# Turning the inner values of the last two experts ahead of the down products before them, in the mixture-of-experts stage of a four-layer diffusion trunk

## The chip, the cores and the metric

One Trainium2 chip, one core of it. The metric is the device time of one execution in microseconds (us), as a median over several runs. All data is 32-bit floating point; most products of the mixture-of-experts stage are computed in the type fp32r, with every operand split into an upper and a lower part.

## The reference

One inference step of a trunk with 4 layers, for 128 context tokens and 256 latent tokens (384 in all) of width 1024. Layer l has a token mixer (gated DeltaNet, grouped-query attention, latent attention, gated DeltaNet) and then a mixture of 16 experts in 4 groups of 4: each token is sent to its best group and to the best two experts in it. Both halves of a layer end in a residual and a layer norm. Cut to the part that the change touches:

```python
def _moe(h, router_w, router_b, w_gate, w_up, w_down):
    ...
    combine = jnp.einsum("tk,tke->te", w, jax.nn.one_hot(e_idx, N_EXPERTS, dtype=jnp.float32)).astype(h.dtype)
    hid = jax.nn.silu(jnp.einsum("td,edf->tef", t, w_gate)) * jnp.einsum("td,edf->tef", t, w_up)
    out = jnp.einsum("tef,efd->td", hid * combine[..., None], w_down)
    return out.reshape(B, N, D)
```

The inner width of an expert is 256. Every layer has its own expert weights.

## The kernel before

Five engines run programs of their own and meet by semaphores: SyncE (SP) issues the weight loads, TensorE (PE) multiplies, ScalarE (ACT) and VectorE (DVE) read the results out of PSUM, GpSimd (POOL) does small side work in the mixers. Weights come through a ring of 8 slots of 1 MB (`ring`, L375); SP's `load` (L662) waits until the slot is free (`ring_free`) and starts the transfer, in the order in which the products use them.

In the mixture-of-experts stage (`moe`, L1550 on TensorE, L2105 on ScalarE, L2839 on VectorE) the tokens of each group are gathered into a block of 128, and the four experts of the group work on this block. The stage is one hand-written list of steps, `MOE_STEPS` (L96 to L117), that TensorE goes through. A step is (kind, group, number):

- U: gate and up products of an expert (`gate_up`, L1538), in 4 pieces of weights with 6 matmuls each. Gate and up values lie in PSUM bank 0 or 1.
- T: the 128 x 256 inner values of an expert are turned (`transpose_hidden`, L1494), by two 128 x 128 transposes into one half of PSUM bank 2: experts with an even number use the first half, those with an odd one the second.
- D: down products of an expert (`down`, L1511), in 2 pieces of weights with 6 matmuls each. They add up in PSUM banks 3 and 4 over the four experts of the group.
- S: a scatter piece (`scatter_piece`, L1523): a quarter of a group's output is put back to its tokens.
- G and W: gathering the blocks, and the weights of the pairs of groups.

Experts of a layer are counted 0 to 15 in what follows: U15 is ("U", 3, 3), T14 is ("T", 3, 2), D13 is ("D", 3, 1). S2 and S3 are the last two scatter pieces of group 2, ("S", 2, 2) and ("S", 2, 3). Down products run two experts behind the gate and up products.

ScalarE and VectorE go through a second list, `MOE_FOLLOW` (L127 to L144), made out of the first one. A U or D step gives one entry P for each piece of weights, and the followers of the other steps (and the "u" of a U step) are collected and put in behind the second piece of the next U or D step. So the order of `MOE_STEPS` also sets the order of work on these two engines. The entries:

- P (pieces counted 0 to 95 in a layer; U15 has 86 to 89, D13 has 90 and 91, D14 92 and 93, D15 94 and 95): ScalarE writes the upper part of 1024 columns of weights (`split_high`, L2084, an activation at L1685, into `e_whi`), VectorE the lower part (`split_low`, L2813, L2817, into `e_wlo`). There are three buffers; ScalarE waits until the piece three before has been multiplied (`wfree`).
- u: ScalarE applies the SiLU to the gate values (L2092), VectorE multiplies by up values and routing weight (`hidden`, L2810), which gives the inner values.
- t: ScalarE copies the turned values out of bank 2 as the upper part (`hidden_t`, L2094, at L1685, semaphore `thi`), VectorE computes the lower part (`hidden_low`, L2819, L2822, semaphore `tlo`), into `e_hidT`. D waits for both.
- s: VectorE adds a scatter piece to the residual, 4 instructions (`scattered`, L2831, L2835).
- y: the group's output is copied in two parts (`y_high` at L1685, `y_low`, L2829).

The last steps of a layer are, on TensorE, `U15 S2 D13 S3 T14 D14 T15 D15` and then four scatter pieces of group 3. The list for the other two engines ends in `P88 P89 P90 P91 u15 s2 P92 P93 s3 t14 P94 P95 t15 y` and the four scatter pieces. Then the layer norm of the layer follows (L793, L1701, L2239), which needs all of them. Matmuls that belong together are written as three lines: L1505, L1508 and L1509 (`split_products`).

Of the kernel before, what the change touches and what calls it, by code (L numbers as in the profile page):

```python
# [29 lines left out]
D = 1024  # L30
KT = D // P
CTX, LAT = 128, 256
T = CTX + LAT
# [10 lines left out]
NE, NG, EPG = 16, 4, 4  # L44
# [51 lines left out]
MOE_STEPS = [("G", 0, m) for m in range(8)]  # L96
for _x in range(NE):
    _group, _turn = divmod(_x - 6, EPG)
    _late = _x >= 6 and _turn < 2
    if _x == 8:  # L100
        MOE_STEPS.append(("W", 1, 0))
    MOE_STEPS.append(("U", _x // EPG, _x % EPG))
    if _x == 0:
        MOE_STEPS.append(("W", 0, 0))
    if _x in (4, 5):
        MOE_STEPS += [("G", 1, 4 * (_x - 4) + m) for m in range(2)]
    if _late:
        MOE_STEPS.append(("S", _group, 2 * _turn))
    if _x >= 2:
        MOE_STEPS.append(("D", (_x - 2) // EPG, (_x - 2) % EPG))  # L110
    if _x in (4, 5):
        MOE_STEPS += [("G", 1, 4 * (_x - 4) + m) for m in range(2, 4)]
    if _late:
        MOE_STEPS.append(("S", _group, 2 * _turn + 1))
    if _x >= 1:
        MOE_STEPS.append(("T", (_x - 1) // EPG, (_x - 1) % EPG))
MOE_STEPS += [("D", 3, 2), ("T", 3, 3), ("D", 3, 3)] + [("S", 3, q) for q in range(4)]  # L117

MOE_UNITS = [(j, e, part) for kind, j, e in MOE_STEPS if kind in "UD" for part in ((0, 1) if kind == "U" else (2,))]

# [240 lines left out]
def trunk(nc, I, O):  # L361

    unit_at, n_units = unit_plan()
    with ExitStack() as ctx:
# [188 lines left out]
        def moe_sems(pre):  # L553
            names = "pick ga ga_ev whi wlo wfree sg hid tr thi tlo yhi ylo sc sc_ev".split()
            return dict(zip(names, sems(" ".join(pre + n for n in names))))

        F = moe_sems("f_")
# [173 lines left out]
        def _(pe):  # L731
# [714 lines left out]
            def gather_piece(l, pair, m):  # L1446

                at = 16 * l + 8 * pair + m
                half, q = divmod(m, 4)
                if m == 0:  # L1450
                    pe.wait_ge(F["pick"], 2 * l + pair + 1)
                    pe.wait_ge(tk_hi, 2 * TT * (l + 1))
                if m == 4:
                    pe.wait_ge(tk_lo, 2 * TT * (l + 1))
                if m >= 2:
                    pe.wait_ge(F["ga_ev"], at - 1)
                out = ps[:, 5 + q % 2, :].rearrange("p (g f c) -> p g f c", g=2, f=2)
                for f in range(2):
                    ft = 2 * q + f
                    for t in range(TT):  # L1460
                        last = mm(out[:, :, f, :], (e_hi, e_lo)[half][:, t, P * ft:P * ft + P], e_pick[:, t, :],  # L1461
                                  start=(t == 0), stop=(t == TT - 1))
                last.then_inc(F["ga"], 1)

            def pair_weights(l, pair, comb):

                pe.wait_ge(comb_ready, l + 1)
                pe.wait_ge(row2_ready, l + 1)
                for g in range(2):
                    at = EPG * (2 * pair + g)  # L1470
                    for t in range(TT):
                        last = mm(ps[:, 7, 96 + 4 * g:100 + 4 * g], e_pick[:, t, P * g:P * g + P].bitcast(F32),
                                  comb[:, t, at:at + EPG], start=(t == 0), stop=(t == TT - 1))
                last.then_inc(cs_mm, 1)
# [19 lines left out]
            def transpose_hidden(S, n, b):  # L1494

                pe.wait_ge(S["hid"], n + 1)
                for m in range(2):
                    last = nc.tensor.transpose(ps[:, 2, 256 * b + P * m:256 * b + P * m + P],
                                               e_hid[:, b, P * m:P * m + P], ident)
                last.then_inc(S["tr"], 1)  # L1500
# [10 lines left out]
            def down(S, n, p, e, k):  # L1511

                b = p % SPLITS
                pe.wait_ge(S["whi"], n + 1)
                pe.wait_ge(S["wlo"], n + 1)
                for y in range(2):
                    cols = slice(512 * y, 512 * y + 512)
                    last = split_products(ps[:, 3 + y, :], [e_hidT[:, e % 2, part, k, :] for part in range(2)],
                                          e_whi[:, b, cols], e_wlo[:, b, cols],
                                          e == 0 and k == 0, e == EPG - 1 and k == 1, S is F and p % 2 == 1 and y == 0)  # L1520
                last.then_inc(S["wfree"], 1)

            def scatter_piece(S, n, q, put, banks, first_of_two):  # L1523

                for ft in (2 * q, 2 * q + 1):
                    if ft % 4 == 0:
                        pe.wait_ge(S["yhi"], 2 * n + ft // 4 + 1)
                        pe.wait_ge(S["ylo"], 2 * n + ft // 4 + 1)
                    if ft >= len(banks):
                        pe.wait_ge(S["sc_ev"], n * KT + (ft - len(banks) + 1))  # L1530
                    elif first_of_two is not None:
                        pe.wait_ge(S["sc_ev"], first_of_two)
                    b = banks[ft % len(banks)]
                    mm(ps[:, b, 0:T], e_yhi[:, P * ft:P * ft + P], put, start=True, stop=False)
                    mm(ps[:, b, 0:T], e_ylo[:, P * ft:P * ft + P], put,
                       start=False, stop=True).then_inc(S["sc"], 1)

            def gate_up(S, n, p, j, e, k):  # L1538

                b = p % SPLITS  # L1540
                pe.wait_ge(S["whi"], n + 1)
                pe.wait_ge(S["wlo"], n + 1)
                for m in range(2):
                    kt, cols = 2 * k + m, slice(512 * m, 512 * m + 512)
                    last = split_products(ps[:, e % 2, :], [e_hs[:, j, part, kt, :] for part in range(2)],
                                          e_whi[:, b, cols], e_wlo[:, b, cols], kt == 0, kt == KT - 1,
                                          S is F and p % 2 == 1 and m == 0)
                last.then_inc(S["wfree"], 1)

            def moe(l):  # L1550
# [50 lines left out]
                with pe.If(crowded > 0):  # L1601
                    with pe.Fori(0, NG) as g:
                        for b in range(2):
                            n = g * 2 + (2 * NG * l + b)
# [30 lines left out]
                for kind, j, e in MOE_STEPS:  # L1635
                    n = NE * l + EPG * j + e
                    if kind == "G":
                        gather_piece(l, j, e)
                    elif kind == "W":
                        pair_weights(l, j, comb)  # L1640
                    elif kind == "U":
                        if e == 0 and j % 2 == 0:
                            pe.wait_ge(F["ga_ev"], 16 * l + 8 * (j // 2) + 8)
                        for k in range(4):
                            p = MOE_PIECE_OF["U", j, e, k]
                            gate_up(F, MOE_PIECES * l + p, p, HS_OF[j], e, k)
                    elif kind == "T":
                        transpose_hidden(F, n, e % 2)
                    elif kind == "D":
                        pe.wait_ge(F["thi"], n + 1)  # L1650
                        pe.wait_ge(F["tlo"], n + 1)
                        for k in range(2):
                            p = MOE_PIECE_OF["D", j, e, k]
                            down(F, MOE_PIECES * l + p, p, e, k)
                    else:
                        n = NG * l + j
                        if e == 0:
                            pe.wait_ge(F["ga_ev"], 16 * l + 16)
                        scatter_piece(F, n, e, e_put[:, j % 2, :], (6, 0, 1, 2) if j == NG - 1 else (5, 6),
                                      n * KT if n else None)  # L1660
# [9 lines left out]
            for l, kind in enumerate(KINDS):  # L1670
                {"gdn": gdn, "gqa": gqa, "mla": mla}[kind](l)
                layer_norm(2 * l, bufh, bufo, lambda k: pe.wait_ge(r_ready, KT * l + k + 1),
                           ("mid", l) if l + 1 < DEPTH else None)
                moe(l)
                layer_norm(2 * l + 1, bufx, bufh, lambda k: pe.wait_ge(F["sc_ev"], KT * (NG * l + NG - 1) + k + 1),
                           ("tail", l) if l + 1 < DEPTH else None)
# [1480 lines left out]
```

## Time and profile before

| | |
|---|---|
| median of 3 runs | 2187.74 us (2181.60 to 2188.81) |
| profiled execution, its own time | 2186.74 us |
| its span | 2184.9 us |
| TensorE busy | 2021.1 us, 92% |
| VectorE busy | 1338.0 us, 61% |
| ScalarE busy | 1034.3 us, 47% |
| granted TensorE clock, mean over the span | 0.973 |
| read from memory | 373.96 MB, 173 GB/s |

In a timeline a row gives the start in us from the start of the span, the duration in us, engine, line and operation, what is written and read, and how many instructions were merged into it (x2); in square brackets stands how long the engine had been idle before it, and what ended that. PEld is TensorE's weight load, which overlaps its matmuls. Ends of matmuls are modelled, and two in a row overlap: their pitch is taken from start to start. The granted clock is 1.00 at TensorE's full 2.4 GHz and 0.50 at 1.2 GHz.

### The profile page before, as it was taken

The page shows a single profiled execution, that of the slowest core. Times are in us where ns is not written, and L with a number is a line of the kernel's source. Part 1 is how long each engine was busy: PE and PEld are TensorE (multiplying, and loading weights), DVE is VectorE, ACT ScalarE, POOL GpSimd, SP SyncE. Part 2 cuts the span into 40 slices and gives each one's busy share as a digit, 9 for nine tenths or more (in the row PEclk, how much of TensorE's full clock was granted, in tenths as well). Part 3 has the DMA queues.
Part 4 walks back from the last instruction along what each step waited for, and adds up shares of the span by engine and source line. Part 5 has one row for each costly group of instructions (what it writes and reads, how often), then busy time and mean ns, then how long its engine had stood idle before and what let it go on. Part 6 is the DMA issues. An engine that isn't in the chain of part 4 may idle for free.

```text
span 2184.9 us, 44966 instructions
## 1 busy us (share of the span) xinstructions
PE 2021.1 (92%) x18880; PEld 1403.4 (64%) x18881; DVE 1338.0 (61%) x2625; ACT 1034.3 (47%) x1783; POOL 246.5 (11%) x363
## 2 busy tenths in 40 slices
PE   6999999898998999899899998998999999988996
PEld 3666666557775675677666665776466666647774
DVE  2656665437896342689822325898656666537896
ACT  3334344226774341676523315766444444326774
POOL 1422222110001000100010001000322232110000
PEclk8999999998999999899999998999999999999998
DMA  9244344345886444488644353888311121125880
GB/s 392 90 152 153 123 146 156 141 156 187 282 322 216 159 172 158 162 309 300 240 150 146 138 190 123 310 303 283 121 46 63 47 70 46 45 80 186 282 303 29
DMA packets 56912, 381.22 MB, mean 174 GB/s; under 512 B 6400, under 2 KB 10624, under 8 KB 12144
## 3 DMA queue, kind: packets, MB, share of 16 engines
q1 hardware_dynamic: 51696, 373.00, 47.7%
q10 hardware_dynamic: 4608, 4.20, 0.6%
q8 instruction: 159, 2.61, 0.5%
q0 software_dynamic: 384, 0.89, 0.1%
q14 instruction: 65, 0.53, 0.1%
HBM read 373.96 MB, written 4.10 MB: 173 GB/s over the span
## 4 chain that ended last, share of the span: by engine, by line
PE 76%; DVE 13%; ACT 5%; issue 4%; DMA 2%; ACTq 0%; SPq 0%; DVEq 0%
PE ps L838 15%; PE ps L1505 6%; DVE e_wlo L2817 5%; PE ps L1509 5%; PE ps L1508 5%; PE ps L788 4%; PE ps L764 4%; PE ps L744 3%; PE ps L979 3%; PE ps L1292 3%; DVE bufx L2835 2%; PE ps L799 2%; PE ps L1461 2%; ACT e_whi L1685 2%; PE ps L1393 2%
## 5 line engine op out<-in xcount | busy, mean ns | idle before, releaser
L2817 DVE TENSOR_TENSOR e_wlo<-ring,e_whi 128x1024 fp32r<-128x1024 f32 x384 | 456.2, 1222 | 90.9 <-ACT e_whi L1685 75.2
L1685 ACT ACTIVATE e_whi<-ring 128x1024 fp32r<-128x1024 f32 x384 | 402.9, 1060 | 117.9 <-PE ps L1509 114.4
L838 PE MATMUL ps<-bufh,ring 128*128 128x384 f32 x1024 | 392.4, 505 | 2.0 <-ACT scratch L1685 0.7
L838 PEld LDWEIGHTS ps<-bufh,ring 128*128 128x128 f32 x1024 | 177.0, 191 | 93.9 <-issue 18.3
L1505 PE MATMUL ps<-e_whi,e_hs 128*128 128x512 f32 x512 | 210.5, 411 | 28.2 <-DVE e_wlo L2817 24.8
L1685 ACT ACTIVATE scratch<-ps 128x384 f32<-128x384 f32 (+6 forms) x311 | 109.0, 368 | 213.2 <-PE ps L838 53.3
L1509 PE MATMUL ps<-e_whi,e_hs 128*128 128x512 f32 x512 | 200.4, 391 | 0.0
L1508 PE MATMUL ps<-e_wlo,e_hs 128*128 128x512 f32 x512 | 200.0, 391 | 0.0
L2946 POOL TENSOR_SCALAR bufx<-bufo,x_gb 128x384 f32<-128x384 f32 x56 | 37.6, 685 | 1072.5 <-DVE bufo L2256 1072.5
L1505 PEld LDWEIGHTS ps<-e_whi,e_hs 128*128 128x128 f32 x512 | 96.0, 188 | 69.1 <-ACT e_whi L1685 43.1
L2349 DVE SCALAR_TENSOR_TENSOR scratch<-scratch,par 128x386 f32<-128x386 f32 x192 | 128.5, 669 | 4.8
L744 PE MATMUL ps<-ring,silc 128*32 128x128 f32 x3072 | 106.3, 293 | 16.5 <-DMA ring<-in_w_ada 16.5
L1685 ACT ACTIVATE scratch<-ps,scratch 128x128 f32<-128x128 f32 x96 | 31.7, 365 | 189.3 <-PE ps L1139 187.7
L1505 PE MATMUL ps<-e_whi,e_hidT 128*128 128x512 f32 x256 | 102.0, 398 | 13.8 <-issue 9.2
L1509 PEld LDWEIGHTS ps<-e_whi,e_hs 128*128 128x128 f32 x512 | 96.1, 188 | 21.6
L1685 ACT ACTIVATE lnt<-ps 128x384 f32<-128x384 f32 x26 | 12.7, 490 | 200.6 <-PE ps L799 178.6
L744 PEld LDWEIGHTS ps<-ring,silc 128*32 128x32 f32 x3072 | 88.6, 117 | 29.7 <-issue 13.7
L1508 PEld LDWEIGHTS ps<-e_wlo,e_hs 128*128 128x128 f32 x512 | 96.4, 188 | 16.3
L979 PEld LDWEIGHTS ps<-scratch 32*32 32x32 f32 x6144 | 65.5, 108 | 55.9 <-issue 40.5
L1508 PE MATMUL ps<-e_wlo,e_hidT 128*128 128x512 f32 x256 | 100.8, 394 | 0.0
L1509 PE MATMUL ps<-e_whi,e_hidT 128*128 128x512 f32 x256 | 100.6, 393 | 0.0
L2235 DVE SCALAR_TENSOR_TENSOR bufh<-ps,mod,bufx 128x128 f32<-128x128 f32 x64 | 23.4, 412 | 118.9 <-PE ps L764 77.3
(312 smaller groups left out, 3490.7 us busy)
## 6 DMA issues: line engine op xcount, KB each, us to landing
ring<-in_moe SPq DMA_DIRECT2D x192, 1024.0 KB, 4.9
ring<-in_w_ada SPq DMA_DIRECT2D x96, 1024.0 KB, 6.8
ring<-in_gdn_w_in SPq DMA_DIRECT2D x32, 1024.0 KB, 7.0
ring<-in_gdn_w_out SPq DMA_DIRECT2D x8, 1024.0 KB, 5.0
ring<-in_gqa_w_in SPq DMA_DIRECT2D x6, 1024.0 KB, 5.1
ring<-in_gqa_w_out SPq DMA_DIRECT2D x4, 1024.0 KB, 6.9
ring<-in_mla_w_out SPq DMA_DIRECT2D x4, 1024.0 KB, 7.7
ring<-in_mla_w_in SPq DMA_DIRECT2D x3, 1024.0 KB, 4.9
```

Of the source, the lines that this page charges most:

```text
L744: last = mm(ps[32 * g:32 * g + 32, bank, 0:P], silc[:, kt, :], w[:, k, g, :], start=(kt == 0), stop=(kt == KT - 1))
L764: last = mm(ps[:, banks[t % len(banks)], 0:T], w[:, t % 2, kt, :], rhs[:, kt, :], start=(kt == 0), stop=(kt == KT - 1))
L788: last = mm(ps[:, banks[t % len(banks)], 0:T], w[:, t % 2, kt, :], bufo[:, kt, :], start=(kt == 0), stop=(kt == KT - 1))
L838: last = mm(ps[:, head_bank(n, m), 0:T], w[:, m % 2, kt, :], bufh[:, kt, :], start=(kt == 0), stop=(kt == KT - 1))
L979: last = mm(ps[quarter(g), bank, at:at + 32], g_inv[a][quarter(g), d, t, :], g_inv[b][quarter(g), d, t, :], start=True, stop=True)
L1292: last = mm(ps[:, bank, 0:T], w[:, pos % 2, kt, :], bufh[:, kt, :], start=(kt == 0), stop=(kt == KT - 1))
L1505: first = mm(out, parts[0], whi, start=start, stop=False)
L1508: mm(out, parts[0], wlo, start=False, stop=False)
L1509: return mm(out, parts[1], whi, start=False, stop=stop)
L1685: return op(out, in_, ACT.Copy, **kw)
L2349: done = stt(acc, g_cin[:, m, tap:tap + CONVW], taps[:, tap:tap + 1], acc, ALU.mult, ALU.add)
L2817: return tt_(e_wlo[:, b, :], w, e_whi[:, b, :].bitcast(F32), ALU.subtract)
```

## The change

T14 and T15 move forward in the list of steps, and TensorE gets one wait more in front of a T step (not for the first expert of a group): that the lower part of the expert before has been computed, since the two halves of bank 2 belong to one bank.

```diff
@@ -104,17 +104,21 @@
         MOE_STEPS.append(("W", 0, 0))
     if _x in (4, 5):
         MOE_STEPS += [("G", 1, 4 * (_x - 4) + m) for m in range(2)]
+    if _x == NE - 1:
+        MOE_STEPS.append(("T", NG - 1, EPG - 2))
     if _late:
         MOE_STEPS.append(("S", _group, 2 * _turn))
     if _x >= 2:
         MOE_STEPS.append(("D", (_x - 2) // EPG, (_x - 2) % EPG))
     if _x in (4, 5):
         MOE_STEPS += [("G", 1, 4 * (_x - 4) + m) for m in range(2, 4)]
+    if _x == NE - 1:
+        MOE_STEPS.append(("T", NG - 1, EPG - 1))
     if _late:
         MOE_STEPS.append(("S", _group, 2 * _turn + 1))
-    if _x >= 1:
+    if 1 <= _x < NE - 1:
         MOE_STEPS.append(("T", (_x - 1) // EPG, (_x - 1) % EPG))
-MOE_STEPS += [("D", 3, 2), ("T", 3, 3), ("D", 3, 3)] + [("S", 3, q) for q in range(4)]
+MOE_STEPS += [("D", 3, 2), ("D", 3, 3)] + [("S", 3, q) for q in range(4)]
@@ -1645,6 +1649,8 @@
                             p = MOE_PIECE_OF["U", j, e, k]
                             gate_up(F, MOE_PIECES * l + p, p, HS_OF[j], e, k)
                     elif kind == "T":
+                        if e:
+                            pe.wait_ge(F["tlo"], n)
                         transpose_hidden(F, n, e % 2)
```

The tail on TensorE becomes `U15 T14 S2 D13 T15 S3 D14 D15`, the list of the other two engines `P88 P89 P90 P91 u15 t14 s2 P92 P93 t15 s3 P94 P95 y`. The order of the weight pieces, and with it the order of the loads, stays as it is. This is so in all four layers.

## Rows read from the trace of the kernel before

**Rows 1.** The page, busy time, share of the span and instructions of each engine.
```profile
PE 2021.1 (92%) x18880; PEld 1403.4 (64%) x18881; DVE 1338.0 (61%) x2625; ACT 1034.3 (47%) x1783; POOL 246.5 (11%) x363
```

**Rows 2.** Timeline of TensorE, tail of layer 3: start us, us, engine, line, operation.
```profile
2141.16 0.33 PE L1534 MATMUL ps<-e_put,e_yhi 128*128 128x384 f32 x1
...
2141.87 0.40 PE L1505 MATMUL ps<-e_whi,e_hidT 128*128 128x512 f32 x1
...
2144.63 0.33 PE L1534 MATMUL ps<-e_put,e_yhi 128*128 128x384 f32 x1
...
2145.33 0.38 PE L1498 MATMUL ps<-con,bufh 128*128 128x128 f32 x2
2148.02 0.47 PE L1505 MATMUL ps<-e_whi,e_hidT 128*128 128x512 f32 x1 [2.31 <-issue]
...
2150.83 0.38 PE L1498 MATMUL ps<-con,bufh 128*128 128x128 f32 x2
2152.42 0.47 PE L1505 MATMUL ps<-e_whi,e_hidT 128*128 128x512 f32 x1 [1.21 <-ACT e_hidT L1685]
```

**Rows 3.** Timeline of VectorE, the same tail.
```profile
2136.65 0.41 DVE L2822 TENSOR_TENSOR e_hidT<-ps,e_hidT 128x256 fp32r<-128x256 f32 x1
...
2142.24 0.48 DVE L2810 SCALAR_TENSOR_TENSOR bufh<-ps,e_cs,bufh 128x256 f32<-128x256 f32 x1
2142.63 1.38 DVE L2835 SCALAR_TENSOR_TENSOR bufx<-ps,mod,bufx 128x128 f32<-128x128 f32 x4
2143.93 2.35 DVE L2817 TENSOR_TENSOR e_wlo<-ring,e_whi 128x1024 fp32r<-128x1024 f32 x2
2146.20 1.39 DVE L2835 SCALAR_TENSOR_TENSOR bufx<-ps,mod,bufx 128x128 f32<-128x128 f32 x4
2147.50 0.41 DVE L2822 TENSOR_TENSOR e_hidT<-ps,e_hidT 128x256 fp32r<-128x256 f32 x1
2147.84 1.22 DVE L2817 TENSOR_TENSOR e_wlo<-ring,e_whi 128x1024 fp32r<-128x1024 f32 x1
```

**Rows 4.** Timeline of ScalarE, the same tail.
```profile
2141.36 0.38 ACT L2092 ACTIVATE bufh<-ps 128x256 f32<-128x256 f32 x1 [0.30 <-PE ps L1509]
2141.64 1.05 ACT L1685 ACTIVATE e_whi<-ring 128x1024 fp32r<-128x1024 f32 x1
2143.46 1.06 ACT L1685 ACTIVATE e_whi<-ring 128x1024 fp32r<-128x1024 f32 x1 [0.76 <-PE ps L1509]
2145.75 0.38 ACT L1685 ACTIVATE e_hidT<-ps 128x256 fp32r<-128x256 f32 x1 [1.23 <-PE ps L1498]
...
2155.44 1.08 ACT L1685 ACTIVATE e_yhi<-ps 128x512 fp32r<-128x512 f32 x2 [3.81 <-PE ps L1509]
```

**Rows 5.** Timeline of TensorE, tail of layer 0: its D14 and D15 begin.
```profile
673.15 0.47 PE L1505 MATMUL ps<-e_whi,e_hidT 128*128 128x512 f32 x1 [2.31 <-issue]
...
677.56 0.47 PE L1505 MATMUL ps<-e_whi,e_hidT 128*128 128x512 f32 x1 [1.21 <-ACT e_hidT L1685]
```

**Rows 6.** Tail of layer 2, TensorE; then engines by window (PEclk, DMA share, GB/s last).
```profile
1518.03 0.47 PE L1505 MATMUL ps<-e_whi,e_hidT 128*128 128x512 f32 x1 [2.29 <-issue]
...
1522.23 0.60 PE L1498 MATMUL ps<-con,bufh 128*128 128x128 f32 x2
...
1519.20:1522.30 3.10, 3.10 (x9) 2.30 (x9) 1.23 (x1) 1.06 (x1) 0.00 (x0) 0.51 0.33 53
```

**Rows 7.** Timeline of TensorE: last product of D13's first half, first of its second.
```profile
2143.03 0.39 PE L1509 MATMUL ps<-e_whi,e_hidT 128*128 128x512 f32 x1
2143.26 0.40 PE L1505 MATMUL ps<-e_whi,e_hidT 128*128 128x512 f32 x1
```

**Rows 8.** Waits of TensorE from 2056 to 2146: total us, times, longest us.
```profile
PE ps L1505 <- DVE e_wlo L2817: 5.6, 7, 1.0
```

**Rows 9.** Engines by window around layer 0's tail, columns as in rows 6.
```profile
670.00:684.00 14.00, 8.87 (x41) 6.81 (x40) 8.16 (x16) 5.35 (x8) 0.00 (x0) 1.00 0.60 219
```

**Rows 10.** Waits of all engines from 684 to 760, TensorE's longest total.
```profile
PEld ps L799 <- ACT bufh L1708: 2.5, 4, 0.7
```

## The prediction

> **What bounds the kernel now.** I read the page first: TensorE is busy for 92% of the span [rows 1], so an idle stretch of TensorE that no other engine fills is lost. Then the timeline of one mixture-of-experts tail, engine by engine, here that of layer 3, from the end of U15 (the gate and up products of expert 15) to the start of D15 (its down products).
>
> TensorE [rows 2] is without a gap from 2141.16 (scatter piece S2) over D13 (2141.87) and S3 (2144.63) to T14 (2145.33). Then it idles: D14 starts at 2148.02, 2.69 us after T14 began; T15 follows at 2150.83, and D15 starts 1.59 us after it, at 2152.42. Both times TensorE waits for its own transposed product to come back through ScalarE (upper part) and VectorE (lower part). What the second engine does meanwhile decides the length: VectorE [rows 3] had the two lower parts of D14's weights (2143.93), the four additions of S3 (2146.20), and only then the lower part of T14 (2147.50, 0.41 us); D14 started 0.11 us after that ended. ScalarE [rows 4] had been done since 2145.75 + 0.38 = 2146.13. So the first wait is VectorE's queue, the second the bare round trip.
>
> The tail ends in work that hangs on D15 alone: ScalarE's copy of the output at 2155.44 had waited 3.81 us for TensorE [rows 4]; scatter and layer norm follow. What D15 gains, the layer gains.
>
> The other layers: layer 0 has the same idle times, 2.31 and 1.21 us [rows 5], and layer 1 repeats them (2.30, 1.18). Layer 2 has the first one too (2.29), but then D14 takes 1522.23 - 1518.03 = 4.20 us instead of 2150.83 - 2148.02 = 2.81, with a granted clock of 0.51 (that is the 1.2 GHz level) from 1519.20 to 1522.30 [rows 2, 6]. TensorE had idled just before it. That layer's tail is 1.39 us longer.
>
> **The change, part by part.**
> *T14 to before S2.* Its input, the inner values of expert 14, was written a whole expert earlier, so nothing holds it; it starts about 2141.16. ScalarE gets to its copy behind the SiLU (2141.36) at about 2141.67 [rows 4]; from T14 to that copy lay 2145.75 - 2145.33 = 0.42 us, which allows 2141.58. VectorE has it directly behind the inner values of expert 15 (2142.24, the next instruction at 2142.63 [rows 3]); a lower part occupies the queue for 2147.84 - 2147.50 = 0.34 us.
> *T15 to between D13 and S3.* Its input is ready at 2142.24 + 0.48 = 2142.72, before D13 ends.
> *VectorE's queue* now sets the end. In its new order, from 2142.63: lower part T14 0.34, additions S2 1.30, weights of D14 2 x 1.14 = 2.27, lower part T15 0.34, additions S3 1.30 (steps of [rows 3]: 2143.93 - 2142.63, 2146.20 - 2143.93, 2147.50 - 2146.20), so the first weights of D15 start at 2142.63 + 5.55 = 2148.18 and end 1.22 later, at 2149.40. From there to the product I add 0.12 (lower part to D14 was 0.11): D15 starts at 2149.52. Nothing in that queue is held from outside: S2 and S3 will have been multiplied by 2142.4 and 2145.9; the upper parts of the weights are early. ScalarE's P93 waits for the first half of D13, as at 2143.46 [rows 4], now some 0.3 later, and VectorE needs it at 2145.4. P94 goes behind T15's copy, at about 2145.7, and VectorE needs it at 2148.2. P95 waits for the first half of D14 (2147.2) and is needed at 2149.3.
> *TensorE's own queue* in the new order: from 2141.16, T14 0.38 (pair's duration, an upper value), S2 0.71, D13 2.76, T15 0.38, S3 0.70, D14 2.81: ready for D15 at 2148.90. So of the two old waits (2.69 + 1.59, less two transposes of 0.38 = 3.52 us) there remains a new one of 0.62 us in front of D15, for a **weight** split that stands behind the additions of S3. The second half of D15 finds its weights at about 2149.3 + 1.22 = 2150.5, before the first half (1.4 us) is over.
> Gain of a tail: 2152.42 - 2149.52 = **2.90 us**; between the bounds 2.6 (each hand-over 0.1 later than I take it) and 3.8 (no new wait, transposes nearly free). Four layers: 11.6.
> *Layer 2's clock.* With the idle time in front of D14 gone I take the slow stretch to go too: 1.39 us more. Bounds: nothing, and 1.39.
> *The added wait.* TensorE waits for the lower part of the expert before in front of 12 transposes of a layer, 48 in all. In the 40 that stay where they were, the down products just before have waited for that same count, so it is met. For T14 it was given by the lower part that began at 2136.65 [rows 3], 4 us earlier. For T15 the count comes from VectorE at 2142.63 + 0.42 = 2143.05 and T15 stands at 2145.0. What a met wait costs, the trace shows where two stand in front of a half of the down products: from the last product of one half to the first of the next 2143.26 - 2143.03 = 0.23 us, the pitch inside a half [rows 7]. I take nothing; bounds 0 and, by the 0.01 to 0.03 that starts scatter by, 48 x 0.03 = 1.4 us. In the full stretches it would partly hide: TensorE waits there for weights 7 times in 90 us [rows 8].
> The Trainium skill ("Advanced Engine Details and Errata", Network/Comms) puts reading a semaphore from a sequencer at 50 to 100 ns, a rule against this change. By it 48 waits would cost 2.4 to 4.8 us and the result would be 2177.1 to 2179.5; the row above shows that the pitch does not open for two of them, so I leave it out of the sum.
> *Queues.* No DMA is added or moved; SP's loads are triggered by down products that come up to 2.9 us sooner, and the DMA engines are 60% busy there [rows 9], so they can follow. No instruction of GpSimd changes.
>
> **Sum**, against the profiled execution, 2186.74 us with a span of 2184.9: 11.6 + 1.4 = 13.0, so 2173.7. The median of the runs shown is 1.0 higher; on that footing **2174.7**. About 0.3%, 6.6 us, is what a measurement of this kernel can tell from no change; its own three runs lie 7 us apart.
>
> **The rivals.**
> *A, the clock (0.10).* The grant falls in some stretches behind idle time and not in others (layer 2 only, though all four tails had the same gap). The moved work may meet it elsewhere: in each of two or three layers one stretch as in layer 2, 1.4 us each. For: everything behind the first tail now runs at another time. Against: the gap becomes shorter everywhere. Result: 2174.7 + 1.4 + 2 x 1.4 = 2178.9. The Trainium skill ("TensorE: Matmul & The Clock Gate", The HAM clock gate) says that the activity watch runs freely and is not tied to the kernel; one tail of four agrees with that.
> *B, VectorE gives half back (0.07).* The new wait in front of D15 is longer by the 1.3 us of additions, because they start late or the copies of ScalarE do. Then 1.6 a layer: 6.4, and 2181.3. Against: all inputs are early by 0.9 us or more.
> *C, the next stage takes it back (0.05).* If the transfers behind the first three tails don't come sooner, the next mixer waits for them, and the last tail's 2.9 alone remains: 2184.8. Against: in the waits of the 76 us behind layer 0's tail TensorE never waits for a transfer; its longest total there is 2.5 us, for ScalarE [rows 10].
> *D, slower (0.04).* The wait in front of the transposes costs what the queue shows at its worst. Place: 48 transposes; it eats the gain from 13.0 / 48 = 0.27 us each and at 0.45 us, between a met wait and one that is not met (5.6 / 7 = 0.8 us [rows 8]), gives 2174.7 + 21.6 = 2196. Only if the count were not met in the steady part could this be.
>
> **How the numbers follow.** The forecast itself (0.74) spans from 2171.0 (no new wait) to 2178.7 (1.4 without the clock, 1.2 for hand-overs, 1.4 for waits); with A and the spread of runs the range is **2169.0 to 2181.5**. It leaves C and D out, and part of B. Faster by over 0.3%: forecast, A and a third of B, 0.86. Within: C, the rest of B, a little of D, 0.11. Slower: 0.03.
>
> **What would show it.** In the timeline of a tail: T14 directly behind U15, T15 behind D13, D14 without idle time behind S3; one wait of 0.6 to 1.0 us in front of D15, ended by VectorE's e_wlo; VectorE going straight from S3's additions to those weights. From the end of U15 (2141.16 before) to D15 8.4 us instead of 11.26. In layer 2 a clock of 1.00 through D14. It would be wrong if D14 still waited, if the wait before D15 were over 1.5 us, if waits of TensorE appeared behind the tail, or if the steady experts grew longer than before.

## The result, and the profile after

The kernel with the change takes 2172.11 us (median of 8 runs, 2168.86 to 2175.47), beside 2184.81 us for the kernel before (8 runs, 2180.86 to 2190.06): 12.7 us less, a ratio of 0.9932 with a 95% interval of 0.9914 to 0.9949. As a gain, the interval is 11.1 to 18.8 us. The forecast was a gain of 13.0 us and 2174.7 us, inside a range of 2169.0 to 2181.5. The forecast started from the 2187.74 us of the first three runs; the median of eight lies 2.9 us lower, which accounts for the 2.6 us between the forecast time and the measured one. The profiled execution took 2172.59 us with a span of 2170.8, against 2186.74 and 2184.9.

The page after, busy time of each engine (compare [rows 1]):

```profile
span 2170.8 us, 45014 instructions
...
PE 2020.3 (93%) x18880; PEld 1404.6 (65%) x18881; DVE 1337.3 (62%) x2625; ACT 1034.0 (48%) x1783; POOL 246.2 (11%) x363
```

The engines do the same work in the same busy time; what went is idle time of TensorE. The page counted 44966 instructions before; the 48 more are the added waits.

The tail of layer 3 on TensorE, timeline after (compare [rows 2]; the line numbers have moved by 4: L1502 is the transpose, L1538 the scatter, L1509 the first of three products):

```profile
2129.88 0.39 PE L1513 MATMUL ps<-e_whi,e_hs 128*128 128x512 f32 x1
2130.11 0.38 PE L1502 MATMUL ps<-con,bufh 128*128 128x128 f32 x2
2130.25 0.42 PE L1538 MATMUL ps<-e_put,e_yhi 128*128 128x384 f32 x1
...
2131.05 0.40 PE L1509 MATMUL ps<-e_whi,e_hidT 128*128 128x512 f32 x1
...
2133.82 0.38 PE L1502 MATMUL ps<-con,bufh 128*128 128x128 f32 x2
2133.95 0.42 PE L1538 MATMUL ps<-e_put,e_yhi 128*128 128x384 f32 x1
...
2134.75 0.40 PE L1509 MATMUL ps<-e_whi,e_hidT 128*128 128x512 f32 x1
...
2137.30 0.39 PE L1513 MATMUL ps<-e_whi,e_hidT 128*128 128x512 f32 x1
2138.45 0.47 PE L1509 MATMUL ps<-e_whi,e_hidT 128*128 128x512 f32 x1 [0.77 <-DVE e_wlo L2823]
```

T14 (2130.11) stands behind U15, T15 (2133.82) behind D13, D14 (2134.75) follows S3 without idle time. One wait is left, 0.77 us in front of D15, and what ends it is VectorE's lower part of the weights (the last product of D14 starts at 2137.30). From the end of U15 to D15 there are 2138.45 - 2130.11 = 8.34 us; before there were 11.26 (2152.42 - 2141.16), and 8.36 was forecast.

VectorE in the same tail (compare [rows 3]):

```profile
2131.16 0.48 DVE L2816 SCALAR_TENSOR_TENSOR bufh<-ps,e_cs,bufh 128x256 f32<-128x256 f32 x1
2131.56 0.41 DVE L2828 TENSOR_TENSOR e_hidT<-ps,e_hidT 128x256 fp32r<-128x256 f32 x1
2131.89 1.39 DVE L2841 SCALAR_TENSOR_TENSOR bufx<-ps,mod,bufx 128x128 f32<-128x128 f32 x4
2133.19 2.35 DVE L2823 TENSOR_TENSOR e_wlo<-ring,e_whi 128x1024 fp32r<-128x1024 f32 x2
2135.46 0.41 DVE L2828 TENSOR_TENSOR e_hidT<-ps,e_hidT 128x256 fp32r<-128x256 f32 x1
2135.79 1.38 DVE L2841 SCALAR_TENSOR_TENSOR bufx<-ps,mod,bufx 128x128 f32<-128x128 f32 x4
2137.09 2.35 DVE L2823 TENSOR_TENSOR e_wlo<-ring,e_whi 128x1024 fp32r<-128x1024 f32 x2
```

It has no idle time from 2131.16 to the end of the weights of D15. From the lower part of T14 to the first weights of D15 it is 2137.09 - 2131.56 = 5.53 us; the sum of steps in the prediction was 5.55.

Over all layers, from the first transpose of a layer to the fold of its last layer norm (starts in TensorE's timeline):

| layer | before | after | gain |
|---|---|---|---|
| 0 | 526.53 to 689.63: 163.10 | 523.82 to 684.08: 160.26 | 2.84 |
| 1 | 926.99 to 1090.08: 163.09 | 924.68 to 1084.98: 160.30 | 2.79 |
| 2 | 1371.38 to 1535.88: 164.50 | 1365.83 to 1526.07: 160.24 | 4.26 |
| 3 | 2001.42 to 2164.47: 163.05 | 1990.28 to 2150.50: 160.22 | 2.83 |

That is 12.7 of the 14.1 us by which the spans differ. The other 1.4 us are a sum of larger pieces of both signs, outside these stretches: ahead of layer 0, before any changed step, the second trace is 2.7 us shorter (523.82 against 526.53); between the layer norms' folds and the next first transposes it is 3.2 us longer behind layer 0 (240.60 against 237.36), 0.5 shorter behind layer 1 and 1.3 shorter behind layer 2; 0.1 shorter at the end. Traces of one and the same kernel differ outside the stretches by as much (1529.8, 1526.7 and 1533.6 us in three traces of the change), so I read no effect of the change in it.

### The profile page after: what moved, and what is told of

It reads as the page before. It is cut to its first block, busy times and chain, and to the rows that moved or that the text cites. A ratio compares the mean times of both kernels' runs of the same rounds, so it can differ in the third digit from the quotient of the medians.

```text
span 2170.8 us, 45014 instructions
## 1 busy us (share of the span) xinstructions
PE 2020.3 (93%) x18880; PEld 1404.6 (65%) x18881; DVE 1337.3 (62%) x2625; ACT 1034.0 (48%) x1783; POOL 246.2 (11%) x363
## 4 chain that ended last, share of the span: by engine, by line
PE 76%; DVE 15%; ACT 5%; issue 3%; DMA 1%; SPq 0%; ACTq 0%; DVEq 0%
PE ps L842 15%; DVE e_wlo L2823 6%; PE ps L1509 6%; PE ps L1513 5%; PE ps L1512 5%; PE ps L792 4%; PE ps L768 4%; PE ps L748 3%; PE ps L983 3%; DVE bufx L2841 3%; PE ps L1296 3%; PE ps L803 2%; ACT e_whi L1691 2%; PE ps L1465 2%; PE ps L1397 2%
## 5 line engine op out<-in xcount | busy, mean ns | idle before, releaser
L1509 PE MATMUL ps<-e_whi,e_hs 128*128 128x512 f32 x512 | 210.9, 412 | 28.1 <-DVE e_wlo L2823 24.5
L1509 PEld LDWEIGHTS ps<-e_whi,e_hs 128*128 128x128 f32 x512 | 96.0, 188 | 68.9 <-ACT e_whi L1691 42.9
L1691 ACT ACTIVATE lnt<-ps 128x384 f32<-128x384 f32 x26 | 12.7, 490 | 199.7 <-PE ps L803 177.7
L1509 PE MATMUL ps<-e_whi,e_hidT 128*128 128x512 f32 x256 | 101.0, 395 | 3.2 <-DVE e_wlo L2823 3.2
```

What stands on the lines that cost most here:

```text
L1509: first = mm(out, parts[0], whi, start=start, stop=False)
L1691: return op(out, in_, ACT.Copy, **kw)
```

## The experiments

All compare with runs of the kernel before on the same chip. "Tail" is the time from the start of the last product of U15 to the first of D15, "stretch" that from the first to the fourteenth transposition of a layer; both come from the starts in TensorE's timeline.

### 1. The wait alone

```diff
                     elif kind == "T":
+                        if e:
+                            pe.wait_ge(F["tlo"], n)
                         transpose_hidden(F, n, e % 2)
```

(with the order of steps of before)

> The order of before, with the added wait of TensorE (lower part of the expert before) in front of 48 transposes. My theory: every one of them is met when TensorE reaches it, so the time is that of before within 1.4 us (48 x 0.03 us at most), and a full stretch of experts in the trace (first to fourteenth transposition of a layer, 133.07 us before, 133.17 us after the change) grows by 0.1 us. Rival, the wait costs 50 to 100 ns of TensorE each: 2.4 to 4.8 us slower than before.

2184.87 us (12 runs) beside 2186.18 (29 runs), ratio 0.9992 (0.9974 to 1.001). The stretch is 133.12, 133.14, 133.12 and 133.12 us, against 133.06 to 133.12 before: it grows by some 0.05. Tails: 11.5 us in layers 0, 2 and 3, 12.8 in layer 1 (the clock, see experiment 6). The waits cost nothing that can be measured.

### 2. The wait written eight times

```diff
-                        if e:
+                        for _ in range(8 if e else 0):
                             pe.wait_ge(F["tlo"], n)
```

(with the change)

> The whole change with the added wait written eight times in front of each of the 48 transposes, so 336 more waits that are met. My theory, a met wait costs TensorE next to nothing: a stretch from the first to the fourteenth transposition of a layer (133.17 us with the change) grows by 0 to 0.7 us and the time by 0 to 3 us. Rival, 50 to 100 ns each: 84 more waits a layer are 4 to 8 us of TensorE's queue; even if the waits for weights (0.8 us an expert) take up a part, the stretch grows by 2 us or more and the time by 10 to 30 us.

2175.02 us (8 runs) beside 2184.09 (16 runs), ratio 0.9957 (0.9936 to 0.9977); its profiled execution is the one of 2169.93. The page counts 45158 instructions, 144 more than the change for 336 waits more. With the change 48 waits had added 48 instructions, here 384 add 192: as if two waits went into one instruction. First the page, then the waits of TensorE from 2040 to 2130 (total us, times, longest), once with eight waits and once with the change:

```profile
span 2168.1 us, 45158 instructions
...
PE ps L1509 <- DVE e_wlo L2823: 5.6, 7, 1.1
```

```profile
PE ps L1509 <- DVE e_wlo L2823: 5.5, 7, 1.0
```

Stretches of 133.18, 133.17, 133.14 and 133.09 us (change: 133.17, 133.19, 133.17, 133.14), tails of 8.57 to 8.60 us (change: 8.57 to 8.59). So 36 more wait instructions in a layer, 30 of them in the stretch and 6 in the tail, change neither by 0.1 us. In the stretch TensorE's waits for weights could hide them. In the tail, from the last product of U15 to the first of D14, there is no idle time that could: that takes 4.83 us in all four layers, and 4.83 to 4.87 with the change. The median is 3 us above that of the change; since no stretch or tail is longer in the trace, I read this as the spread of runs, 12 us wide in this kernel (the trace is that of its fastest run, so the 3 us themselves are not explained). The rival, 50 to 100 ns for each wait, falls: the 36 instructions alone would be 1.8 us a layer at 50 ns, and the 6 in front of D14 0.3 us where less than 0.05 is seen.

### 3. T14 alone

```diff
-    if _x == NE - 1:
-        MOE_STEPS.append(("T", NG - 1, EPG - 1))
...
-MOE_STEPS += [("D", 3, 2), ("D", 3, 3)] + [("S", 3, q) for q in range(4)]
+MOE_STEPS += [("D", 3, 2), ("T", 3, 3), ("D", 3, 3)] + [("S", 3, q) for q in range(4)]
```

(against the change)

> The change with T15 left where it was, behind D14; T14 moved on all engines. My theory, VectorE's queue sets the end: from the start of T14 its queue reads inner values to 1.45, lower part T14 to 1.78, S2 to 3.08, weights of D14 to 5.35, additions S3 to 6.65, weights of D15 to 8.93, lower part T15 to 9.34, so D15 starts 9.45 us behind the end of U15, against 11.26 before and 8.34 with the whole change. Gain 1.8 us a tail, 7.2 in all (up to 1.4 more where the clock stays up in layer 2). Rival, the two idle stretches are independent round trips: moving T14 takes the first one whole (2.3 us a tail, 9.2 in all) and T15 would be worth the remaining 0.6.

2178.65 us (12 runs) beside 2186.18, ratio 0.9966 (0.9952 to 0.998): 7.5 us faster. All four tails are 9.66 or 9.67 us, against 11.49 before: 1.8 us each, the forecast of VectorE's queue and not the rival's 2.3. VectorE and then TensorE in layer 3:

```profile
2137.53 1.38 DVE L2839 SCALAR_TENSOR_TENSOR bufx<-ps,mod,bufx 128x128 f32<-128x128 f32 x4
2138.83 2.35 DVE L2821 TENSOR_TENSOR e_wlo<-ring,e_whi 128x1024 fp32r<-128x1024 f32 x2
2141.10 0.41 DVE L2826 TENSOR_TENSOR e_hidT<-ps,e_hidT 128x256 fp32r<-128x256 f32 x1
```

```profile
2139.45 0.38 PE L1500 MATMUL ps<-con,bufh 128*128 128x128 f32 x2
2141.61 0.47 PE L1507 MATMUL ps<-e_whi,e_hidT 128*128 128x512 f32 x1 [1.78 <-DVE e_hidT L2826]
```

The wait in front of D14 is gone, and the one in front of D15 has grown, from 1.21 us before [rows 2] to 1.78: the lower part of T15 is now last in a VectorE queue without gaps. The two waits are not worth their lengths one by one, since they stand in the same queue.

### 4. T14 early on TensorE only

```diff
+_t, _s = ("t", 3, 2, None), ("s", 2, 3, None)
+MOE_FOLLOW.remove(_t)
+MOE_FOLLOW.insert(MOE_FOLLOW.index(_s) + 1, _t)
 MOE_PIECES = _p
```

(against experiment 3)

> As the kernel with T14 alone moved, but ScalarE and VectorE read T14's result where they did before, behind the additions of S3; only TensorE's transposes move, by 4.2 us. My theory, VectorE's place in its queue ended the wait in front of D14: nothing is gained, D14 still waits 2.3 us and the time is that of before within 1.4 us. Rival, the wait was the round trip of the transposed values: with the transposes 4.2 us earlier D14 waits no more, 9 us faster than before.

2183.36 us (12 runs) beside 2186.18, ratio 0.9984 (0.9966 to 1.0001). Nothing of the gap is gained: D14 starts 7.06 to 7.08 us behind the last product of U15 in all layers, as before (7.07 to 7.08). Layer 3, the transposes and ScalarE's copy, then VectorE, then TensorE:

```profile
2134.28 0.38 PE L1503 MATMUL ps<-con,bufh 128*128 128x128 f32 x2
2137.78 0.36 ACT L1692 ACTIVATE e_hidT<-ps 128x256 fp32r<-128x256 f32 x1
```

```profile
2139.30 1.39 DVE L2842 SCALAR_TENSOR_TENSOR bufx<-ps,mod,bufx 128x128 f32<-128x128 f32 x4
2140.60 0.41 DVE L2829 TENSOR_TENSOR e_hidT<-ps,e_hidT 128x256 fp32r<-128x256 f32 x1
```

```profile
2141.11 0.47 PE L1510 MATMUL ps<-e_whi,e_hidT 128*128 128x512 f32 x1 [2.27 <-issue]
```

The transposes ran at 2134.28 and ScalarE's copy was done at 2138.14, and D14 still waits 2.27 us, until 0.1 us after VectorE has had its turn at them (2140.60 + 0.41). By itself the move on TensorE gains nothing: the wait is ended by the place in the list of the followers. The move is still needed for the full gain. In the kernel before, ScalarE's copy was done at 2146.13, so with the transposes left in place VectorE could have come to the lower part at most 1.37 us earlier than 2147.50 (an estimate from [rows 3] and [rows 4]; that order was not run).

### 5. The additions of S3 behind the last weights

```diff
 MOE_FOLLOW += _open
+_s = ("s", 2, 3, None)
+MOE_FOLLOW.remove(_s)
+MOE_FOLLOW.insert(MOE_FOLLOW.index(("y", 3, 3, None)), _s)
 MOE_PIECES = _p
```

(with the change; TensorE's order stays)

> The whole change, and VectorE's four additions of S3 put behind the second piece of D15's weights instead of in front of the first. My theory, the one wait left in front of D15 (0.77 us idle in the trace after) is VectorE's weight split standing behind these additions: VectorE would finish D15's first weights 1.4 us before TensorE is through with D14, D15 starts 0.9 us earlier in each tail, 3.7 us less than the change, 16 less than before. The additions end some 1.5 us before the output of the last group is copied, so nothing is late for them. Rival, the wait comes from ScalarE's upper parts or the buffers of weights: the time is that of the change, and the wait in front of D15 or of its second half stays at 0.7 us or more.

2169.11 us (6 runs) beside 2186.18, ratio 0.9923 (0.9902 to 0.9945), all four tails 7.6 us. It was run twice more, each time with the change on the same chip:

> The change itself, for a second trace and its time beside the kernel with the additions late. From the end of U15 to D15 8.6 us in all four tails, none of them with a lowered clock; 12.7 us below before, within 3 us.

> The change with the additions of S3 put behind the last weights of D15, once more, for its time on the same chip as the change. My theory: 3.9 us below the change (four tails of 0.97 us, as in its first trace), so 16 to 17 us below before. Rival: the first trace's longer span elsewhere (clock at the 1.2 GHz level for 104 us in all against 90) belongs to it, and it is no faster than the change.

2171.89 us for the change (7 runs) and 2170.09 for this kernel (6 runs), beside 2184.09 for before; ratios 0.9938 (0.9916 to 0.996) and 0.9917 (0.9893 to 0.9942).

> The change once more, for its time beside the kernel with the additions late: 12 to 13 us below before; its four tails 8.6 us each, clock at full speed in all.

> The additions of S3 behind the last weights of D15, beside the change on the same chip. By the traces (7.6 us a tail against 8.6) 3.9 us below the change; the two earlier medians were 3.0 and 1.8 us below it. Rival: that is the spread of runs, and this median is at or above the change's.

2172.16 us (6 runs) and 2166.84 us (6 runs), beside 2185.02; ratios 0.9929 (0.9904 to 0.9954) and 0.9916 (0.9887 to 0.9945). VectorE and TensorE in the tail of layer 3 of this last trace:

```profile
2128.01 0.42 DVE L2831 TENSOR_TENSOR e_hidT<-ps,e_hidT 128x256 fp32r<-128x256 f32 x1
2128.34 1.22 DVE L2826 TENSOR_TENSOR e_wlo<-ring,e_whi 128x1024 fp32r<-128x1024 f32 x1
2129.98 1.23 DVE L2826 TENSOR_TENSOR e_wlo<-ring,e_whi 128x1024 fp32r<-128x1024 f32 x1 [0.42 <-ACT e_whi L1694]
2131.12 1.39 DVE L2844 SCALAR_TENSOR_TENSOR bufx<-ps,mod,bufx 128x128 f32<-128x128 f32 x4
2133.64 1.29 DVE L2838 TENSOR_TENSOR e_ylo<-ps,e_yhi 128x512 fp32r<-128x512 f32 x2 [1.14 <-ACT e_yhi L1694]
```

```profile
2129.83 0.39 PE L1516 MATMUL ps<-e_whi,e_hidT 128*128 128x512 f32 x1
2130.05 0.39 PE L1512 MATMUL ps<-e_whi,e_hidT 128*128 128x512 f32 x1
...
2134.59 0.41 PE L1541 MATMUL ps<-e_put,e_yhi 128*128 128x384 f32 x1 [1.61 <-DVE e_ylo L2838]
```

D15 (2130.05) now follows D14 at the pitch of 0.22 us, without a wait. VectorE's idle time has moved to where it costs nothing, and the additions end 1.1 us before VectorE is wanted for the output. In all three traces every tail is 7.56 to 7.64 us against 8.57 to 8.60 with the change: 1.0 us each, 4 us in all. The three medians lie 3.0, 1.8 and 5.3 us below that of the change (for the first, the change had run in another set). The traces show the gain; the intervals of the two ratios overlap. In the two sets that have both kernels the means differ by 3.1 and 4.3 us; weighted together that is 3.6 us with an interval of about 0.4 to 6.7 (my estimate from the single runs), so by the runs alone the gain is just clear of nothing and its size is open.

### 6. The kernel before, a second trace

> The kernel before, for a second trace of its four tails. So far each trace with a 2.3 us gap in front of D14 (the kernel before, the wait alone, T14 on TensorE alone) showed the clock at the 1.2 GHz level in exactly one tail of four, layer 2, 1 and 1, for 1.3 to 1.4 us of loss; traces with the gap closed showed none in twelve tails. If the gap is the cause, this trace shows such a tail again, in whichever layer; if it belongs to layer 2, it is layer 2 again.

One execution, 2190.57 us. Tails of 11.47, 11.47, 12.86 and 11.49 us: the long one is in layer 2 again. Timeline of TensorE there:

```profile
1519.13 0.38 PE L1498 MATMUL ps<-con,bufh 128*128 128x128 f32 x2
1521.83 0.47 PE L1505 MATMUL ps<-e_whi,e_hidT 128*128 128x512 f32 x1 [2.31 <-issue]
1526.03 0.60 PE L1498 MATMUL ps<-con,bufh 128*128 128x128 f32 x2
```

D14 takes 1526.03 - 1521.83 = 4.20 us again [rows 6]. And in the trace of the wait alone, in layer 1 (there D15 at 1082.02, tail 12.78 us):

```profile
1076.32 0.77 PE L1505 MATMUL ps<-e_whi,e_hidT 128*128 128x512 f32 x1 [2.31 <-issue]
1080.65 0.38 PE L1498 MATMUL ps<-con,bufh 128*128 128x128 f32 x2
```

Put together: four traces have the 2.3 us gap in front of D14 (before, before again, experiments 1 and 4), and each has one tail of four that is 1.3 to 1.4 us longer, layer 2, 2, 1 and 1. Eight traces have not (the change three times, experiments 2 and 3, experiment 5 three times), and none of their 32 tails is. It doesn't belong to a layer, so the gap is what it goes with. The lower level set in 1.2 us after D14 had started in the two traces of the kernel before, and 0.1 to 0.2 us before it started in the other two; the shorter wait in front of D15 (1.2 us) was never followed by one. Why one tail of four and not another, no run shows.

## Why the prediction was right, point by point

- *VectorE's queue ended the first wait.* Shown by experiment 4: with the transposes ahead of S2, 7 us before D14, and the turns of ScalarE and VectorE left in place, nothing is gained.
- *The second wait as the bare round trip.* Not quite. In the trace of before, ScalarE's copy of T15 was done at 2151.25 + 0.38 = 2151.63, and VectorE took the lower part at 2151.90, straight behind a weight split of D15. Some 0.25 us of that wait were VectorE's queue too. The sum did not use this, since it adds up the new queue.

```profile
2151.25 0.38 ACT L1685 ACTIVATE e_hidT<-ps 128x256 fp32r<-128x256 f32 x1 [0.52 <-PE ps L1498]
```

```profile
2150.76 1.23 DVE L2817 TENSOR_TENSOR e_wlo<-ring,e_whi 128x1024 fp32r<-128x1024 f32 x1 [1.71 <-ACT e_whi L1685]
2151.90 0.42 DVE L2822 TENSOR_TENSOR e_hidT<-ps,e_hidT 128x256 fp32r<-128x256 f32 x1
```

- *T14 and T15 start where I put them, and ScalarE is never late.* As forecast. ScalarE copied T14 at 2130.59 and T15 at 2134.24 (0.38 us each), and was through 0.6 and 0.8 us before VectorE came to them.
- *5.55 us of VectorE's queue from the lower part of T14 to the first weights of D15.* Measured 5.53. D15 at 8.34 us behind the end of U15, forecast 8.36; a gain of 2.91 us a tail (11.48 to 8.57, from the last product of U15), forecast 2.90.
- *A new wait of 0.62 us in front of D15.* It is 0.77 us by the row. From start to start, as the prediction counted, it is more: the last product of D14 starts at 2137.30, and at a pitch of 0.23 us D15 could have followed at 2137.53, 0.92 us before 2138.45. The part that was off is TensorE's own queue: from T14 to D14 I had 4.93 us and it took 2134.75 - 2130.11 = 4.64. A pair of transposes took 0.13 to 0.14 us and not 0.38 (2130.25 - 2130.11, 2133.95 - 2133.82), and a scatter piece behind it 0.80 and not 0.70. It did not move the end, since VectorE's queue set it. Experiment 5 shows that this wait is the weight split behind the additions: 1.0 us of tail went with them. The tail without any wait is 3.9 us shorter than before; my upper bound for it was 3.8.
- *The added wait at nothing, bounded by 1.4 us.* Experiments 1 and 2: nothing that shows. In the first trace the layers gained 2.79 to 2.84 and not 2.9, since the stretch was 133.14 to 133.19 us instead of 133.06 to 133.12; but other traces, the second one of before too (133.11 to 133.19), have the same length, so this is not the wait's. The 50 to 100 ns that the Trainium skill ("Advanced Engine Details and Errata", Network/Comms) gives for reading a semaphore are not seen in front of matmuls here.
- *Layer 2's clock, 1.39 us more.* Layer 2 gained 4.26 us, 1.4 more than the others. That the slow stretch goes with the gap holds in twelve traces. But its place in layer 2 was chance, and taking the full 1.39 was luck: I knew one trace, and that each of the four traces with the gap would have exactly one such tail came out only later.
- *The next stages give nothing back.* In the first pair of traces the stage behind layer 0 is 3.2 us longer after the change, which looks like rival C. It does not hold up: the same stage takes 237.4 to 239.4 us in the four traces with the gap (mean 238.6) and 236.7 to 240.7 in the eight without (mean 239.0). All time outside the four stretches of the table is 1531.3 us in the mean of the former and 1530.6 in the mean of the latter, with single traces from 1523.9 to 1538.5. So the gain of the tails stays, within the 14.6 us by which this rest varies. That the forecast of 13.0 and the 12.7 between the medians agree to 0.3 us is luck to that extent; the medians of the three sets give gains of 12.7, 12.2 and 12.9.
- *The rivals.* A (the clock falls at the moved work): in none of the changed tails. Elsewhere the clock does vary: the mean over the profiled spans lies between 0.971 and 0.978, with the kernel before and with the change alike. The spread between runs goes with it: of the 29 runs of the kernel before in one set the fastest (2175.57 us) had a mean of 0.980 and the slowest (2201.24) one of 0.969, and a line through all 29 falls by 1.7 us for each 0.001. What sets it in one run and not in another, no run shows. B: the new wait was 0.77 us, not 2. C and D did not occur (above, and experiments 1 and 2).

Not tried: the order of the change without the added wait. The two halves of one PSUM bank would be written by TensorE and read by another engine without a guard. The Trainium skill ("PSUM — Partial Sum Buffer", PSUM bank collisions raise a hardware error) says that such accesses are not held apart by the hardware; no run here shows it.

## What to carry to other kernels

Where an engine waits for a short result from another one, read what the other engine did during the wait: if it was busy with its own list, the place of the short step in that list is the thing to move, and moving the producer alone may be worth nothing, as here. Then add up the follower's queue in its new order, instruction by instruction from the starts in the timeline: here it gave the new end to 0.1 us, and it named the next thing to move (here additions that nobody waited for, in front of weights that somebody did). Two waits that stand in one such queue must not be added up one by one.

## What the runs showed of the hardware that I had not expected

A wait that is already met costs TensorE nothing that can be seen in a stream of matmuls: 144 more wait instructions left stretches and tails the same within 0.1 us, and 6 of them in a part of the tail without idle time within 0.05 us. And a gap of 2.3 us of idle time was followed by a stretch at the 1.2 GHz level in 4 of 16 tails (1.3 to 1.4 us lost each); in the other 32 tails, with gaps of 0.8 us, of 1.8 us (experiment 3) or none (experiment 5), it never was. Four cases are too few for a limit between 1.8 and 2.3 us.
